# Sparse attention's queries: 512, 320 and 240 columns instead of 512, 512 and 48, a norm for each chunk, moved conversions, and identity products on TensorE

## The reference, cut to what matters

```python
def _nsa_mixer(u, kv, w_qg, q_norm, w_o, rel_bias):
    qg = u @ w_qg                                   # 1024 query columns, then 48 gate columns
    q = _rmsnorm(qg[..., :1024].reshape(..., 64), q_norm)     # a norm of each head of 64
    gates = jax.nn.sigmoid(qg[..., 1024:].reshape(..., 3))
    o_cmp, p_slc = _compressed_branch(q, k_cmp, v_cmp, rel_bias)   # 15 blocks of keys
    o_slc = _selected_branch(q, k_slc, v_slc, idx, rel_bias)
    o_win = _window_branch(q, k_win, v_win, rel_bias)
    o = gates[..., 0:1] * o_cmp + gates[..., 1:2] * o_slc + gates[..., 2:3] * o_win
    return o.reshape(bsz, seq, D_MODEL) @ w_o
```

## Time and profile before

| | |
|---|---|
| median of 3 runs | 1479.25 us (1477.46 to 1480.97) |
| profiled execution, its time and its span | 1478.31 us, 1476.5 us |
| TensorE busy, of the span | 1403.1 us, 95% |
| VectorE, ScalarE, GpSimd busy | 859.2, 807.9, 328.8 us |
| chain that ended last, by engine | PE 85%, DVE 9%, ACT 3%, issue 2%, POOL 1% |
| mean granted clock of TensorE | 0.973 |

### The profile page before, as it was taken

How to read it: one execution, slowest core, us unless ns; L and a number is a source line. 1 busy time by engine, 2 the same in 40 slices (tenths; PEclk the granted TensorE clock), 3 DMA queues, 4 the chain that set the end, 5 groups by cost and what they waited for, 6 DMA issues and landing times.

```text
span 1476.5 us, 22108 instructions
## 1 busy us (share of the span) xinstructions
PE 1403.1 (95%) x7386; PEld 1159.7 (79%) x7386; DVE 859.2 (58%) x1248; ACT 807.9 (55%) x1322; POOL 328.8 (22%) x375
## 2 busy tenths in 40 slices
PE   7998989999879999978899999999999989999998
PEld 6887878887758888767788888888888866788887
DVE  5536665446666645669655555555555569455554
ACT  6766476674665454433664444765444548464442
POOL 2011000011159989967210000010000015000000
PEclk9998999999989999978999999999999979999999
DMA  9532535531456555310785655477655420366661
GB/s 335 171 95 72 214 110 165 160 108 45 171 128 188 184 164 160 100 29 16 239 251 185 191 190 185 159 147 224 195 187 185 134 72 2 114 190 188 191 188 54
DMA packets 170861, 224.73 MB, mean 152 GB/s; under 512 B 15880, under 2 KB 113264, under 8 KB 170784
## 3 DMA queue, kind: packets, MB, share of 16 engines
q1 hardware_dynamic: 168016, 217.27, 45.9%
q0 software_dynamic: 2288, 6.15, 2.6%
q10 hardware_dynamic: 480, 0.29, 0.1%
HBM read 221.16 MB, written 1.44 MB: 151 GB/s over the span
## 4 chain that ended last, share of the span: by engine, by line
PE 85%; DVE 9%; ACT 3%; issue 2%; POOL 1%; DVEq 0%; POOLq 0%; ACTq 0%
PE psum L1609 15%; PE psum L1597 11%; PE psum L1599 11%; PE psum L1598 11%; PE psum L386 8%; PE psum L388 8%; PE psum L387 8%; PE psum L523 2%; PE psum L412 2%; DVE w_lo L338 1%; PE psum L1636 1%; PE psum L532 1%; PE psum L2787 1%; PE psum L2587 1%; PE psum L1623 1%
## 5 line engine op out<-in xcount | busy, mean ns | idle before, releaser
L1796 DVE TENSOR_TENSOR w_lo<-w_raw,w_hi 128x1024 fp32r<-128x1024 f32 x216 | 284.3, 1318 | 287.3 <-ACT w_hi L1730 287.1
L1730 ACT ACTIVATE w_hi<-w_raw 128x1024 fp32r<-128x1024 f32 x216 | 229.0, 1061 | 308.9 <-PE psum L1599 217.1
L338 DVE TENSOR_TENSOR w_lo<-w_raw,w_hi 128x1024 fp32r<-128x1024 f32 (+4 forms) x191 | 225.7, 1209 | 121.7 <-ACT w_hi L330 120.4
L1597 PE MATMUL psum<-w_hi,x_hi 128*128 128x512 f32 x704 | 280.7, 399 | 1.5 <-DVE x_lo L438 0.7
L1599 PE MATMUL psum<-w_hi,x_lo 128*128 128x512 f32 x704 | 275.3, 391 | 0.0
L1598 PE MATMUL psum<-w_lo,x_hi 128*128 128x512 f32 x704 | 274.8, 390 | 0.0
L330 ACT ACTIVATE w_hi<-w_raw 128x1024 fp32r<-128x1024 f32 (+4 forms) x191 | 193.2, 1039 | 107.9 <-PE psum L388 63.8
L386 PE MATMUL psum<-w_hi,x_hi 128*128 128x512 f32 (+5 forms) x608 | 232.2, 382 | 3.8 <-DVE x_lo L2920 2.3
L388 PE MATMUL psum<-w_hi,x_lo 128*128 128x512 f32 (+5 forms) x608 | 227.6, 374 | 0.0
L387 PE MATMUL psum<-w_lo,x_hi 128*128 128x512 f32 (+5 forms) x608 | 227.4, 374 | 0.0
L1599 PEld LDWEIGHTS psum<-w_hi,x_lo 128*128 128x128 f32 x704 | 132.6, 188 | 28.5
(11 more groups left out here) (413 smaller groups left out, 1830.5 us busy)
## 6 DMA issues: line engine op xcount, KB each, us to landing
w_raw<-in_ffn_w_in SPq DMA_DIRECT2D x352, 256.0 KB, 3.2
w_raw<-in_ffn_w_out SPq DMA_DIRECT2D x176, 256.0 KB, 2.8
w_raw<-in_w_in SPq DMA_DIRECT2D x88, 256.0 KB, 3.5
w_raw<-in_w_out SPq DMA_DIRECT2D x32, 256.0 KB, 3.8
w_raw<-in_w_kv SPq DMA_DIRECT2D x24, 256.0 KB, 2.9
w_raw<-in_mem_wk SPq DMA_DIRECT2D x16, 256.0 KB, 5.5
w_raw<-in_mem_wv SPq DMA_DIRECT2D x16, 256.0 KB, 5.1
w_raw<-in_mem_wq SPq DMA_DIRECT2D x16, 256.0 KB, 6.0
```

The lines of the kernel that those rows point to most:

```text
L338: nc.vector.tensor_tensor(w_lo[:, s, 0:size(u)], w_raw[:, s, 0:size(u)], w_hi[:, s, 0:size(u)].bitcast(F32), ALU.subtract).then_inc(lo_rea ...
L1597: nc.tensor.matmul(o, xh, whi, start=(kt == 0), stop=False)
L1730: nc.scalar.activation(w_hi[:, s, :], w_raw[:, s, :], ACT.Copy).then_inc(hi_ready, 1)
L1796: nc.vector.tensor_tensor(w_lo[:, s, :], w_raw[:, s, :], w_hi[:, s, :].bitcast(F32), ALU.subtract).then_inc(lo_ready, 1)
```

## The change

Five things change.

1. `Q_HEADS`: the 1072 columns of w_qg are cut as 8 heads (512 columns), 5 heads (320) and 3 heads with the 48 gate columns (240), instead of 512, 512 and 48. The units stay nine in number: 4, 3 (960, 960 and 640 columns wide) and 2 (960 each), instead of 4, 4 and 1.
2. Each of the three chunks has a norm of its own, with its mean, square root and reciprocal. The multiplications are `nsa.qn0` and `nsa.qn1` from chunk 0, `nsa.qn2` (5 heads) from chunk 1, `nsa.qn3` (3 heads) from chunk 2.
3. The gates' sigmoid moves behind the last copy of turned heads.
4. The conversions of w_o's first five units move. Before, all five stood ahead of the compressed scores' work, on VectorE in one row. Now three stand there, the fourth behind the third pair's copy on ScalarE and between the two halves of the compressed scores' work on VectorE, the fifth in the attention, ahead of copy 24 on ScalarE and of scale 28 on VectorE.
5. `pe_busy`: products of the identity by two copies of the identity (256 columns, f32), 19 in all: 3 ahead of the wait for `nsa.qn3`, 2 ahead of each half of the compressed scores, and 3, 2 and 7 behind the scores of jobs 0, 1 and 2. Nobody reads what they write.

```diff
+Q_HEADS = ((0, 8), (8, 5), (13, 3))
...
-        for c in range(2):
-            chunk(f"qg.{c}", d["w_qg"][0], 512 * c, 512)
-        chunk("qg.gates", d["w_qg"][0], NH * HD, 3 * NH)
+        for c, (first, n) in enumerate(Q_HEADS):
+            chunk(f"qg.{c}", d["w_qg"][0], HD * first, HD * n + (3 * NH if c == 2 else 0))
...
+        def pe_busy(pe, b, n):
+            for _ in range(n):
+                nc.tensor.matmul(two_heads(psum[:, b, 0:2 * P]), ident[:], bc(ident[:], 1, 2), start=True, stop=True)
...
             for j in range(m):
                 pe_scores(pe, tag, j, jobs[j])
+                if j in waiting:
+                    waiting[j]()
...
-            pe_chunk(pe, "qg.gates")
+            pe_chunk(pe, "qg.2")
             pe_heads(pe, "nsa.q", lambda t, i: q_nat2[:, t, i * P:(i + 1) * P], NH // 2, P,
-                     lambda a: [f"nsa.qn{a}"])
-
-            pe.wait_ge(*when("nsa.qT3"))
-            pe.wait_ge(*when("cmp.kT1"))
+                     lambda a: [f"nsa.qn{a}"], busy={3: 3})
+
             for t in range(T):
                 b = take(pe, "T", f"cmp.scores{t}")
+                pe_busy(pe, b, 2)
+                if t == 0:
+                    pe.wait_ge(*when("nsa.qT3"))
+                    pe.wait_ge(*when("cmp.kT1"))
...
-            pe_attend(pe, "nsa.sm", jobs, pv, between={0: compressed_turn, 1: compressed_out})
+            pe_attend(pe, "nsa.sm", jobs, pv, between={0: compressed_turn, 1: compressed_out},
+                      waiting={j: lambda n=n: pe_busy(pe, o_banks[1][1], n) for j, n in enumerate((3, 2, 7))})
...
-            for c in (0, 1, "gates"):
-                if c == "gates":
-                    act_root(act, "nsa.q", RI_Q, 32)
-                hi_parts(act, chunk_end(f"qg.{c}") + RING - 1)
+            for c, (first, n) in enumerate(Q_HEADS):
+                if c < 2:
+                    hi_parts(act, chunk_end(f"qg.{c}") + RING - 1)
                 act.wait_ge(used, chunk_end(f"qg.{c}"))
...
+                if c < 2:
+                    act_root(act, f"nsa.q{c}", q_rows(c)[0], q_rows(c)[1])
+            q_out = lambda pairs: heads_out(act, "act", "nsa.q", qT, NH // 2, P, "nsa.qT", scale=gcol["qk"][:, 0:1], pairs=pairs)
+            q_out(range(2))
+            act_root(act, "nsa.q2", q_rows(2)[0], q_rows(2)[1])
+            q_out([2])
+            hi_parts(act, chunk_end("qg.2") + RING - 2)
+            q_out([3])
+            for t in range(T):
+                nc.scalar.activation(gate[:, t], bank(f"qg.2.t{t}")[:, 3 * HD:3 * HD + 3 * NH].rearrange("p (a x) -> p a x", x=3), ACT.Sigmoid,
...
-            act_attend(act, "nsa.sm", nsa_jobs(), between={0: compressed_turned})
+            act_attend(act, "nsa.sm", nsa_jobs(), between={0: compressed_turned, 24: lambda: hi_parts(act, chunk_end("qg.2") + RING - 1)})
...
                 dve.wait_ge(*when(f"nsa.qsq{c}"))
-                nc.vector.tensor_reduce(ss[:, :, 8 * c:8 * c + 8], sc, AX.X, ALU.add).then_inc(*done("nsa_dve", f"nsa.qss{c}"))
-                if c == 0:
-                    lo_parts(dve, chunk_end("qg.gates"))
-            dve_mean(dve, "nsa.q", RI_Q, 32, HD, "nsa.qss1")
-            dve_rstd(dve, "nsa.q", RI_Q, 32)
...
-            lo_parts(dve, chunk_end("qg.gates") + RING - 1)
+                nc.vector.tensor_reduce(ssq[:, i:i + rows], squares[c], AX.X, ALU.add).then_inc(*done("nsa_dve", f"nsa.qss{c}"))
+                dve_mean(dve, f"nsa.q{c}", i, rows, HD, f"nsa.qss{c}")
+                dve_rstd(dve, f"nsa.q{c}", i, rows)
...
+            lo_parts(dve, chunk_end("qg.1") + RING - 1)
...
+                if t == 0:
+                    lo_parts(dve, chunk_end("qg.2") + RING - 2)
...
-            dve_attend(dve, "nsa.sm", nsa_jobs(), between={0: compressed_scaled})
+            dve_attend(dve, "nsa.sm", nsa_jobs(), between={0: compressed_scaled, 28: lambda: lo_parts(dve, chunk_end("qg.2") + RING - 1)})
```

More of the change, by code:

```diff
@@ L602, in act_turned, with pe_attend @@
                                  ACT.Copy).then_inc(*done("softmax_act", f"{tag}.pt_sb{j}", frees=(f"{tag}.pt{j}",)))
-        def pe_attend(pe, tag, jobs, pv, between={}):
+        def pe_attend(pe, tag, jobs, pv, between={}, waiting={}):
             n, m = len(jobs), AHEAD + 1
@@ L858, in pe_mem_kv, with pe_heads @@
             pe_heads(pe, f"memk{l}", lambda t, i: mk_nat[:, t, i * P:(i + 1) * P], MEM_H, P, [f"memk{l}.nat1"])
-        def pe_heads(pe, tag, src, n, width, ready):
+        def pe_heads(pe, tag, src, n, width, ready, busy={}):
             for a in range(n // 2):
+                if a in busy:
+                    b = take(pe, "T", f"{tag}.hb{a}")
+                    pe_busy(pe, b, busy[a])
                 for x in ready(a) if callable(ready) else ready if a == 0 else ():
                     pe.wait_ge(*when(x))
-                b = take(pe, "T", f"{tag}.hb{a}")
+                if a not in busy:
+                    b = take(pe, "T", f"{tag}.hb{a}")
                 for i in range(2):
@@ L870, in pe_heads, with heads_out @@
                 last.then_inc(*done("lift_pe", f"{tag}.headed{a}"))
-        def heads_out(eng, who, tag, dst, n, width, label, scale=None):
-            for a in range(n // 2):
+        def heads_out(eng, who, tag, dst, n, width, label, scale=None, pairs=None):
+            for a in range(n // 2) if pairs is None else pairs:
                 eng.wait_ge(*when(f"{tag}.headed{a}"))
@@ L2737, in dve_kv_rest, with q_rows @@
             dve_rstd(dve, "cmp.k", RI_KC, 1)
+        def q_rows(c):
+            return RI_Q + T * Q_HEADS[c][0], T * Q_HEADS[c][1]
         def nsa_jobs():
@@ L2829, in act_nsa @@
                     b = bank(f"qg.{c}.t{t}")
[L2830 to L2836 removed]
+                    nc.scalar.activation(q_nat2[:, t, HD * first:HD * (first + n)], b[:, 0:HD * n], ACT.Copy, scale=r
+                                         ).then_inc(*done("nsa_act", f"nsa.q{c}{t}", frees=((f"qg.{c}.t{t}",) if c < 2 else ())))
+                if c < 2:
[8 more added lines that the diff above has]
+                nc.scalar.activation(gate[:, t], bank(f"qg.2.t{t}")[:, 3 * HD:3 * HD + 3 * NH].rearrange("p (a x) -> p a x", x=3), ACT.Sigmoid,
+                                     scale=rstd[:, RI_QN + t:RI_QN + t + 1]
+                                     ).then_inc(*done("nsa_act", f"nsa.gate{t}", frees=(f"qg.2.t{t}",)))
             for t in range(T):
@@ L2862, in dve_nsa @@
             lo_parts(dve, chunk_end("qg.0") + RING - 1)
-            sq = (sm_p.rearrange("p a b (c x) -> p (a b c) x", x=HD), sm_t.rearrange("p a b (c x) -> p (a b c) x", x=HD))
+            p16, t16 = [x.rearrange("p a b (c x) -> p (a b c) x", x=HD) for x in (sm_p, sm_t)]
+            squares = (p16, t16[:, 0:10], t16[:, 10:16])
             q4 = q_nat2.rearrange("p t (a x) -> p t a x", x=HD)
-            ss = ssq[:, RI_Q:RI_Q + 32].rearrange("p (t a) -> p t a", t=T)
-            for c in range(2):
-                qc, sc = q4[:, :, 8 * c:8 * c + 8, :], sq[c].rearrange("p (t a) x -> p t a x", t=T)
+            for c, (first, n) in enumerate(Q_HEADS):
+                i, rows = q_rows(c)
+                qc = q4[:, :, first:first + n, :]
@@ L2868, in dve_nsa @@
                 dve.wait_ge(*when(f"nsa.q{c}1"))
-                nc.vector.tensor_tensor(sc, qc, qc, ALU.mult).then_inc(*done("nsa_dve", f"nsa.qsq{c}"))
+                nc.vector.tensor_tensor(squares[c].rearrange("p (t a) x -> p t a x", t=T), qc, qc, ALU.mult).then_inc(*done("nsa_dve", f"nsa.qsq{c}"))
                 dve.wait_ge(*when(f"nsa.qsq{c}"))
-                nc.vector.tensor_reduce(ss[:, :, 8 * c:8 * c + 8], sc, AX.X, ALU.add).then_inc(*done("nsa_dve", f"nsa.qss{c}"))
-                if c == 0:
-                    lo_parts(dve, chunk_end("qg.gates"))
@@ L2874, in dve_nsa @@
-            dve_mean(dve, "nsa.q", RI_Q, 32, HD, "nsa.qss1")
-            dve_rstd(dve, "nsa.q", RI_Q, 32)
-            dve.wait_ge(*when("nsa.q.rstd"))
-            rq = rstd[:, RI_Q:RI_Q + 32].rearrange("p (t a) -> p t a", t=T)
-            for c in range(4):
-                q = q4[:, :, 4 * c:4 * c + 4, :]
-                nc.vector.tensor_tensor(q, q, bc(rq[:, :, 4 * c:4 * c + 4], 3, HD), ALU.mult
-                                        ).then_inc(*done("nsa_dve", f"nsa.qn{c}"))
-            lo_parts(dve, chunk_end("qg.gates") + RING - 1)
+                nc.vector.tensor_reduce(ssq[:, i:i + rows], squares[c], AX.X, ALU.add).then_inc(*done("nsa_dve", f"nsa.qss{c}"))
@@ new lines, in dve_nsa @@
+                dve_mean(dve, f"nsa.q{c}", i, rows, HD, f"nsa.qss{c}")
+                dve_rstd(dve, f"nsa.q{c}", i, rows)
+                dve.wait_ge(*when(f"nsa.q{c}.rstd"))
+                rq = rstd[:, i:i + rows].rearrange("p (t a) -> p t a", t=T)
+                for x in ((0, 4), (4, 8)) if c == 0 else ((0, n),):
+                    q = qc[:, :, x[0]:x[1], :]
+                    nc.vector.tensor_tensor(q, q, bc(rq[:, :, x[0]:x[1]], 3, HD), ALU.mult
```

(1 more changed line is left out.)

7 lines of the change are left out of this document (removed).

## The result

The changed kernel takes 1469.9 us (median of 6 runs, 1466.04 to 1470.88), the kernel before 1479.16 in the same comparison (6 runs, 1475.23 to 1480.97). The profiled execution took 1466.04 us and is the fastest of the six.

What follows compares the result with a forecast made beforehand. TensorE, busy 95% of the span, was taken as the bound, with 20.4 us of the stage at 1.2 GHz. A lead of 7.1 us less 1.1 for conversions gave -6.0: 1473.3 from 1479.25, range 1470.8 to 1476.8.

Steps and rivals of the forecast that it cites:

- a sign of being wrong: TensorE still in the 7 identity products when job 2's bias is done; forecast to end with 0.1 us to spare.
- the clock term of the sum: Compressed scores to compressed output: clock held at 1.00; scores 3.6 us instead of 5.16, output 3.8 instead of 5.49.
- The low stretch at w_o: Behind the attention: 3.3 us at half clock costing 1.65; its vanishing counted only in the range's low end.
- The conversions in the attention: Ahead of copy 24 (ScalarE) and scale 28 (VectorE): 1.1 us taken back, bounds 0 and 2.2.
- One low stretch remains: Between 1183.8 and 1189 or at the compressed scores: 3.4 us at half clock cost at most 1.7; 1475.0, chance 0.22.
- The clock falls as before: Low from 1187.5 to 1190.9 and from 1194.3 on, lead gone at the jobs' row; 1479 to 1480, chance 0.12.
- Products at 1.2 GHz throughout: Identity products not counted as activity, half clock from 1187.5 to 1211; +5.4, so 1484.6, chance 0.05.
- The conversions at full length: Moved conversions in the attention cost 2.2 us instead of 1.1; 1474.4, or 1475 if a slot is in use; chance 0.09.
- Its own two items: Range's low end: conversions hidden (-1.1) and the half-clock stretch behind the attention gone (1.65), taken as 2.6 together.

## Why the forecast came out wrong in size

**The course inside the stage was right.** Each point, counted from the mark, forecast against measured: chunk 2's products end at +9.0, +9.1; `nsa.qn3` is ready at +13.6, +13.4; the last copy of heads ends at +14.8, +14.9; the compressed scores end at +19.5, +19.5; scores 3 start at +26.4, +26.6; the jobs' row starts at +32.0, +32.5; the first product with w_o at +82.1, +82.2. (The forecast figures are the prediction's times less its profile's mark, 1174.07.) The 48 products of 320 columns take 7.04 us (1166.06 to 1173.10), 0.147 each, those of 240 0.112 (0.145 and 0.115 were taken). The 7 identity products last from 1192.76 to 1195.98, 0.23 us for each of their 14 instructions where 0.215 was taken, and end 0.3 us behind the bias that releases scores 3 (forecast: 0.1 to spare). The prediction had named that as a sign of being wrong; it came, and cost at most these 0.3 us. The first three stand in the wait for `nsa.qn3`, 0.67 us of which are left.

**The step that failed is the clock term of the sum**: "If these products hold it at 1.00, the compressed scores take 3.6 us (5.16 were 2.1 at full and 3.1 at half clock", with the break in the low clock from 1190.9 to 1194.3 taken as a feature of the kernel. It was one of the execution. In the three other profiles the low stretch goes from about +13 to +40.5 without a break. Against those, the same changed kernel gains more at three places: the compressed scores start at +18.45 instead of +18.16 (0.3), the compressed scores take 7.03 instead of 5.16 (1.9), their output 5.97 instead of 5.49 (0.5). The stage shrinks from 90.77 to 82.19, by **8.6** and not 5.9. The mechanism stands; the term was 2.6 too small.

**Why the one execution looked normal.** It took 1478.31 us, near the median, and the prediction leaned on that. Two departures cancelled in it: its mark came at 1174.07, 2.4 us behind the mean of all 14 profiles (1171.7, between 1169.05 and 1174.11; the program up to there is the same but for the 0.13 us), and its stage was 2.65 us shorter than the usual. Being near the median as a whole, it said nothing of its parts.

The 14 marks fall into three groups, by two places in the first 350 us where the clock is low in some executions:

```profile
139.60:149.80 10.20, 10.05 (x36) 8.65 (x36) 7.07 (x18) 6.39 (x26) 4.70 (x3) 0.50 0.27 54
```

```profile
139.10:149.30 10.20, 8.95 (x61) 7.56 (x62) 6.81 (x18) 7.60 (x29) 4.44 (x3) 1.00 0.27 56
342.70:346.10 3.40, 3.40 (x12) 2.84 (x13) 2.63 (x8) 2.78 (x13) 3.24 (x3) 0.50 0.00 0
```

The first row is of the profile before, the two others of the changed kernel's first. Five profiles have 10.2 us at half clock from about 139 on, and marks of 1173.1 to 1174.1; five have them from about 342 on instead, and 1171.2 to 1172.5; four have only 3.4 us there, and 1169.05 to 1169.40. The kernel before, the changed kernel and the form with products in the last wait each stand in two of the groups, so the group is not set by the change. What sets it is open.

**The low stretch at w_o.** The range left 1.65 us for its vanishing, together with hidden conversions. All four profiles of the kernel before have it. Of the changed kernel's three, one has it and two have not; from w_o to the end they take 1.5 us more or less accordingly (214.2 or 212.7 us from there). It was absent in three of the five profiles whose clock had stayed at 1.00 through the stage and that have no products in the last wait, and never where the clock had fallen in the stage (seven profiles). What decides between the three and the two is open. On average this gives some 0.9 us.

**The sum anew**: 8.6 in the stage (some 7.9 if the short form of the low stretch is counted at one in four) and 0.9 at w_o make 8.8 to 9.5 us; the 0.13 ahead of the mark come on top. Measured were 9.3 in the first comparison and 8.3 in the last. The sum was made when the result was known; what supports its main term is that two further profiles of the kernel before repeated the 90.8.

**The conversions in the attention** were put at 1.1 us and cost 0.7 (49.54 against 48.83): the direction was right, and 0.4 of slack more was found.

**The rivals.** *One low stretch remains*: it didn't appear in any of three profiles, though only 4 of some 9 us from 1189 on are identity products, which was the reason given for it. *The clock falls as before*: that is what happens without the products, so these and not the chunks hold it. *Products at 1.2 GHz throughout*: refuted, also for transposes. The argument against it, that a fuller row had brought the clock back at 1211.3, was not needed: here the clock never fell. *The conversions at full length*: refuted by the 0.7.

**The range.** Its low end added the cases of the changed kernel only. It held nothing for a kernel before whose usual stage is longer than the one that was read, though the three times shown (1477.46 to 1480.97) vary by 3.5 us with the same program. Its own two items were also added up short: 1.1 and 1.65 are 2.75 and not 2.6, which puts the low end at 1470.5. Even that lies above 1469.9.

## What to carry to other kernels

Where the gain is low clock that goes away, the size of the term is the length of the low stretches in the usual execution, and one profile doesn't tell that: profile the kernel before three or four times, count from a mark ahead of the change, and widen the range on the side of the gain if only one is at hand. In a row of short work whose waits bring the clock down, fill the waits with products that nobody reads, sized to end when the wait ends: with only the early waits filled a third of the gain was gone (1472.7 us), with none of them more than half (1474.9). Where the low stretch begins is seen from the granted clock in a profile; how short a wait can be left empty was not tried. A conversion that must move belongs where the engines wait for something else (ahead of copy 1 and scale 3 it cost nothing, ahead of copy 24 and scale 28 0.7 us).

## What the runs showed that I had not expected

- The granted clock fell at about +13 in all four executions of the kernel before, stayed low in three and came back for 3.4 us in the fourth, with the same program; that alone moved the stage by 2.6 us.
- Transposes of the identity kept the clock at 1.00 exactly as f32 products of the same total length did (stage 82.18 us, and 82.18 to 82.20).
- Nearly the same first 1170 us of program took between 1169.05 and 1174.11 us in 14 profiles, in three groups by where the clock was low in the first 350 us, while the stage with products repeated to 0.02 us (82.20, 82.19, 82.18): with the clock at 1.00 throughout, it didn't vary.
- A half-clock stretch can move without a change of the work ahead of it: in the form with identity products only it began inside the 48-column product, at +10.9, where the kernel before, with the same instructions up to there, had it at +13.1 to +13.4.
